# A third of the first projection by channel tiles, with the modulation weights in eight pieces

## What is computed

```
mod = silu(c) @ ada_w + ada_b                    # (1, 3072)
shift, scale, gate = split(mod, 3)
h = rms_norm(x, norm_g) * (1 + scale) + shift    # (1024, 1024)
p = h @ w_in                                     # (1024, 6152)
sb_q, sb_k, sb_v, ... = split(p)                 # 512 columns each
out = x + gate * (y @ w_out)                     # y: two attention branches, merged
```

## Time and profile before

| | us |
|---|---|
| median of 3 runs | 1090.92 |
| lowest, highest | 1087.15, 1091.58 |
| the profiled execution | 1092.36 |
| its span, first to last instruction | 1090.6 |
| mean granted TensorE clock, share of full | 0.945 |
| PE busy | 985.8 (90%) |
| DVE busy | 548.4 (50%) |
| ACT busy | 294.5 (27%) |
| POOL busy | 232.5 (21%) |

### The profile page before, as it was taken

The page is one execution under the profiler, slowest core; times in us unless marked ns, Lnnn a source line. Parts: engine busy times, 40 slices in busy tenths (PEclk is TensorE's granted clock), DMA queues, the critical chain, the costliest instruction groups (busy, mean ns, idle before and its releaser), DMA issues.

```text
span 1090.6 us, 14498 instructions
## 1 busy us (share of the span) xinstructions
PE 985.8 (90%) x5931; PEld 832.7 (76%) x5931; DVE 548.4 (50%) x768; ACT 294.5 (27%) x700; POOL 232.5 (21%) x112
## 2 busy tenths in 40 slices
PE   2279999869999899999979998899999969999998
PEld 2279999757787688888757886688888858788886
DVE  5888644667778344444034227033335472854522
ACT  2331111326777432122611100123233311111000
POOL 0241130060000021211213020200011253685000
PEclk9589999859999899999989998899999979999999
DMA  8906100231101112121221342511212944345331
GB/s 273 346 7 193 41 1 1 83 112 33 33 21 35 47 39 58 39 59 33 64 57 51 130 120 91 132 42 47 69 49 68 322 141 135 116 142 185 108 100 64
DMA packets 110763, 100.59 MB, mean 92 GB/s; under 512 B 17927, under 2 KB 90208, under 8 KB 110442
## 3 DMA queue, kind: packets, MB, share of 16 engines
q1 hardware_dynamic: 110698, 99.67, 30.0%
HBM read 73.44 MB, written 24.12 MB: 89 GB/s over the span
## 4 chain that ended last, share of the span: by engine, by line
PE 72%; DVE 10%; DMA 8%; ACT 3%; issue 3%; POOL 3%; SPq 1%; ACTq 0%; DVEq 0%
PE psum L688 32%; PE psum L263 7%; PE psum L264 7%; PE psum L265 7%; PE psum L902 3%; DMA sg<-z_scratch 3%; PE psum L887 3%; DMA w3raw<-in_w_in 2%; PE psum L873 2%; DMA ada<-in_ada_w 2%; DVE macc L465 1%; PE psum L875 1%; DVE blocks L1549 1%; PE psum L1216 1%; DVE stick L993 1%
## 5 line engine op out<-in xcount | busy, mean ns | idle before, releaser
L688 PE MATMUL psum<-hhi,w3hl 128*128 128x512 f32 x1152 | 389.4, 409 | 23.5 <-issue 19.6
L688 PEld LDWEIGHTS psum<-hhi,w3hl 128*128 128x128 f32 x1152 | 222.7, 193 | 74.6 <-issue 24.6
L688 PE MATMUL psum<-hlo,w3hl 128*128 128x512 f32 x576 | 229.6, 399 | 0.0
L678 POOL TENSOR_TENSOR w3hl<-w3raw,w3hl 128x1024 fp32r<-128x1024 f32 x44 | 107.5, 2444 | 536.5 <-DVE w3hl L672 536.5
L688 PEld LDWEIGHTS psum<-hlo,w3hl 128*128 128x128 f32 x576 | 111.9, 194 | 23.3 <-issue 2.2
L263 PE MATMUL psum<-w1hi,hhi 128*128 128x256 f32 (+1 forms) x384 | 110.4, 287 | 16.2 <-ACT hst L386 7.8
L672 DVE CAST w3hl<-w3raw 128x1024 fp32r<-128x1024 f32 x44 | 35.8, 814 | 157.8 <-DMA w3raw<-in_w_in 137.5
L264 PE MATMUL psum<-w1lo,hhi 128*128 128x256 f32 (+1 forms) x384 | 109.4, 285 | 0.0
L265 PE MATMUL psum<-w1hi,hlo 128*128 128x256 f32 (+1 forms) x384 | 109.3, 285 | 0.0
L993 DVE TENSOR_TENSOR_SCAN stick<-stick,zero 128x1024 f32<-128x1024 f32 (+7 forms) x64 | 91.8, 1473 | 19.1 <-ACT stick L945 18.9
L263 PEld LDWEIGHTS psum<-w1hi,hhi 128*128 128x128 f32 x384 | 74.1, 193 | 16.6 <-issue 16.6
(11 more groups left out here) (211 smaller groups left out, 1450.7 us busy)
## 6 DMA issues: line engine op xcount, KB each, us to landing
w3raw<-in_w_in SPq DMA_DIRECT2D x36, 512.0 KB, 4.2
z_scratch<-zst SPq DMA_DIRECT2D x48, 256.0 KB, 2.3
ada<-in_ada_w SPq DMA_DIRECT2D x8, 1024.0 KB, 8.3
sg<-z_scratch SPq DMA_DIRECT2D x8, 1024.0 KB, 4.9
w1raw<-in_w_in SPq DMA_DIRECT2D x6, 1024.0 KB, 6.8
xrow<-in_x SPq DMA_DIRECT2D x8, 512.0 KB, 7.5
adag<-in_ada_w SPq DMA_DIRECT2D x8, 512.0 KB, 4.1
zraw<-z_scratch SPq DMA_DIRECT2D x8, 512.0 KB, 6.3
```

Source lines behind the costliest of these rows:

```text
L678: nc.gpsimd.tensor_tensor(w3lo[:, i % 2], w3raw[:], cast(w3hi[:, i % 2]), ALU.subtract).then_inc(w3_lo, 1)
L688: t = nc.tensor.matmul(out_, a[:, i % 2, kt, :], moving[b][:, kt, 512 * half:512 * half + 512], start=(ends[0] and kt == k0 and m == 0), s ...
```

## The change

- `x` is loaded whole, in four loads of 1 MB, ahead of all weights; squared, scaled and turned whole, and kept turned in `hturn`, which lies where `hlo` will be. ACT copies it there from PSUM.
- The weights of shift and scale come in eight pieces, one for each channel tile (kt): 128 columns of shift and 128 of scale, two loads of 512 KB, in two buffers. For each, DVE makes a weighted sum 256 wide (`channel_sums`), PE two sums over partitions (`modulation`), and DVE shift and gain of that channel tile (`gains`).
- ACT makes h of a channel tile twice from `hturn` (128x1024): once in float32 and once as `hhi`. DVE makes the low part (`low_h`). POOL has nothing to do in phase 0.
- Chunks 0 and 1 are done together, 512 columns wide, by channel tile: seven row tiles in seven PSUM banks, then the eighth row tile alone. Bank 7 holds the modulation sums. Their weights come in two halves of the contraction; the high part is made by ACT (`high_w`), the low part by DVE (`low_w`).
- Chunk 2 has buffers of its own, where `hst` and `macc` were, and its low part is made by DVE. Chunks 3 to 5 go as before, with the other buffers; `high_1` of chunk 3 waits for the end of the first pair, `r_mm` 8.
- SP loads the weights of chunks 2 and 3 at the end of `sp_0`, those of 4 and 5 between the gate's weights.

```diff
+            for i in range(ST // 2):
+                sp.dma_start(xrow[:, 2 * i:2 * i + 2, :], x_v[:, 2 * i:2 * i + 2, :]).then_inc(x_in[i], 16)
+            def load_ada(kt):
+                if kt >= 2:
+                    sp.wait_ge(mod_part, kt - 1)
+                for part in range(2):
+                    n0 = D * part + P * kt
+                    sp.dma_start(ada[:, kt % 2, :, part], ada_v[:, :, n0:n0 + P]).then_inc(ada_in[kt % 2], 16)
+            load_ada(0)
+            for half in range(2):
+                for ch in range(2):
+                    kts = slice(KT // 2 * half, KT // 2 * (half + 1))
+                    sp.dma_start(w1raw[:, ch, kts, 0:256], w_v[:, kts, 256 * ch:256 * ch + 256]).then_inc(w1_in[half], 16)
+                if half == 0:
+                    load_ada(1)
+            for kt in range(2, KT):
+                load_ada(kt)
+            load_w1(sp, 2)
+            load_w1(sp, 3)
...
+            for half in range(2):
+                for kt in range(KT):
+                    for i in range(ST // 2):
+                        st = ST // 2 * half + i
+                        if kt == 0:
+                            pe.wait_ge(xn_ok, st + 1)
+                        if i == 0 and KT * half + kt >= FIRST:
+                            pe.wait_ge(xt_ok, KT * half + kt - FIRST + 1)
+                        t = nc.tensor.transpose(turned(half, kt)[:, P * i:P * i + P], xrow[:, st, P * kt:P * kt + P], ident[:, :])
+                    t.then_inc(xt_mm, 1)
+        def modulation(pe, kt):
+            pe.wait_ge(mod_part, kt + 1)
+            if kt:
+                pe.wait_ge(mod_ok, kt)
+            for part in range(2):
+                t = nc.tensor.matmul(bank(7)[:, part:part + 1], macc[:, kt % 2, P * part:P * part + P], ones[:, 0:1],
                                      start=True, stop=True)
             t.then_inc(mod_mm, 1)
...
+            def keep_turned(half, kt):
+                act.wait_ge(xt_mm, KT * half + kt + 1)
+                nc.scalar.copy(hturn[:, kt, 512 * half:512 * half + 512], turned(half, kt)).then_inc(xt_ok, 1)
+            def high_w(half):
+                act.wait_ge(w1_in[half], 32)
+                kts = slice(KT // 2 * half, KT // 2 * (half + 1))
+                nc.scalar.copy(w1hi[:, :, kts, 0:256], w1raw[:, :, kts, 0:256]).then_inc(w1_hi, 1)
+            def modulate(kt):
+                act.wait_ge(mod_ok, kt + 1)
+                act.wait_ge(xt_ok, KT + kt + 1)
+                if kt >= 2:
+                    act.wait_ge(hlo_ok, kt - 1)
+                for h in (hst[:, kt % 2], hhi[:, kt]):
+                    t = nc.scalar.activation(h, hturn[:, kt], ACT.Identity, bias=shift[:, kt:kt + 1],
+                                             scale=g1[:, kt:kt + 1])
+                t.then_inc(hf_ok, 1)
             norm(0)
             norm(1)
+            for kt in range(KT):
+                keep_turned(0, kt)
+            for kt in range(KT // 2):
+                keep_turned(1, kt)
+            high_w(0)
             modulate(0)
+            for kt in range(KT // 2, KT):
+                keep_turned(1, kt)
+            high_w(1)
+            for kt in range(1, KT):
+                modulate(kt)
...
+            def channel_sums(kt):
+                dve.wait_ge(ada_in[kt % 2], 32 * (kt // 2 + 1))
+                if kt >= 2:
+                    dve.wait_ge(mod_mm, kt - 1)
+                weighted_sum(dve, macc[:, kt % 2].rearrange("p (a b) -> p a b", a=2), ada[:, kt % 2], mod_part)
+            def gains(kt):
+                dve.wait_ge(mod_mm, kt + 1)
+                a, b = V_AB + KT + kt, V_AB + kt
+                nc.vector.tensor_tensor(shift[:, kt:kt + 1], bank(7)[:, 0:1], paramT[:, b:b + 1], ALU.add)
+                link(dve, dve_chain, nc.vector.tensor_tensor(ab1[:, kt:kt + 1], bank(7)[:, 1:2], paramT[:, a:a + 1], ALU.add))
+                nc.vector.scalar_tensor_tensor(out=g1[:, kt:kt + 1], in0=ab1[:, kt:kt + 1], scalar=1.0,
+                                               in1=paramT[:, V_NG + kt:V_NG + kt + 1], op0=ALU.add,
+                                               op1=ALU.mult).then_inc(mod_ok, 1)
+            def low_h(kt):
+                dve.wait_ge(hf_ok, kt + 1)
+                nc.vector.tensor_tensor(hlo[:, kt], hst[:, kt % 2], cast(hhi[:, kt]), ALU.subtract).then_inc(hlo_ok, 1)
+            def low_w(half):
+                dve.wait_ge(w1_hi, half + 1)
+                kts = slice(KT // 2 * half, KT // 2 * (half + 1))
+                nc.vector.tensor_tensor(w1lo[:, :, kts, 0:256], w1raw[:, :, kts, 0:256], cast(w1hi[:, :, kts, 0:256]),
+                                        ALU.subtract).then_inc(w1_lo, 1)
...
             scale_rows(dve, 0)
             scale_rows(dve, 1)
+            channel_sums(0)
+            gains(0)
+            channel_sums(1)
+            low_w(0)
+            for kt in range(KT):
+                low_h(kt)
+                if kt + 1 < KT:
+                    gains(kt + 1)
+                if kt + 2 < KT:
+                    channel_sums(kt + 2)
+                if kt == 1:
+                    low_w(1)
...
+        def slot_free(eng, ch):
+            if ch == 2:
+                eng.wait_ge(hlo_ok, KT)
+            else:
+                eng.wait_ge(r_mm, ST if ch < NCH - 1 else 3 * ST)
...
+        def first_chunks(pe):
+            def tile(st, kt):
+                w = [t[:, 0:2, kt, 0:256] for t in (w1hi, w1lo)]
+                return three(bank(st), hhi[:, kt, P * st:P * st + P], hlo[:, kt, P * st:P * st + P], w[0], w[1],
+                             kt == 0, kt == KT - 1)
+            modulation(pe, 0)
             for kt in range(KT):
+                if kt + 1 < KT:
+                    modulation(pe, kt + 1)
+                pe.wait_ge(w1_hi, 1 + (kt >= KT // 2))
+                pe.wait_ge(w1_lo, 1 + (kt >= KT // 2))
+                pe.wait_ge(hf_ok, kt + 1)
+                pe.wait_ge(hlo_ok, kt + 1)
+                for i in range(FIRST):
+                    st = (i + 2) % FIRST
+                    if kt == 0:
+                        pe.wait_ge(xt_ok, min(KT + 2 + i, 2 * KT))
+                    t = tile(st, kt)
                     if kt == KT - 1:
                         t.then_inc(r_mm, 1)
+            pe.wait_ge(mod_ok, KT)
+            for kt in range(KT):
+                t = tile(FIRST, kt)
+            t.then_inc(r_mm, 1)
         def pe_1(pe):
+            first_chunks(pe)
+            for ch in range(2, NCH):
                 pe.wait_ge(w1_hi, ch + 1)
                 pe.wait_ge(w1_lo, ch + 1)
+                for st in range(ST):
+                    n = (ch - 1) * ST + st
+                    pe.wait_ge(r_ok, n - 2 if ch == 2 and st < 4 else n - 3)
                     for kt in range(KT):
+                        w = [t[:, kt, 0:width_1(ch)] for t in (high_of(ch), low_of(ch))]
                         t = three(bank(n % 4)[:, 0:width_1(ch)], hhi[:, kt, P * st:P * st + P],
+                                  hlo[:, kt, P * st:P * st + P], w[0], w[1], kt == 0, kt == KT - 1)
                     t.then_inc(r_mm, 1)
+            pe.wait_ge(r_ok, ST)
...
+            for st in range(ST):
+                act.wait_ge(r_mm, st + 1)
+                t = (st + 2) % FIRST if st < FIRST else st
+                nc.scalar.copy(rows[:, 0, t, :], bank(t)).then_inc(r_ok, 1)
+            for n in range(ST, (NCH - 1) * ST):
+                ch, st = n // ST + 1, n % ST
                 act.wait_ge(r_mm, n + 1)
                 if ch == NCH - 1:
                     nc.scalar.copy(ba[:, st, :], bank(n % 4)[:, 256:256 + WB])
                 nc.scalar.copy(rows[:, ch // 2, st, 256 * (ch % 2):256 * (ch % 2) + 256],
                                bank(n % 4)[:, 0:256]).then_inc(r_ok, 1)
+                if n in (2 * ST + 3, 4 * ST + 3):
+                    act.wait_ge(ss1_ok, 1 if n < 4 * ST else 2)
...
-            high_1(dve, 1)
+            high_1(dve, 2)
+            low_2(dve)
+            high_1(dve, 3)
             dve.wait_ge(par1_in, 64)
             nc.vector.scalar_tensor_tensor(out=gain[:, 2], in0=gain[:, 0], scalar=float(HD) ** -0.5, in1=gain[:, 1],
                                            op0=ALU.mult, op1=ALU.mult)
             for g in range(GG // 2):
                 gate_sum(g)
-            high_1(dve, 2)
+            high_1(dve, 4)
             for g in range(GG // 2, GG):
                 gate_sum(g)
             dve.drain().then_inc(gacc_ok, 1)
-            dve.wait_ge(r_ok, 2 * ST)
-            high_1(dve, 3)
+            dve.wait_ge(r_ok, ST)
             squares(0)
             normalize(0)
-            high_1(dve, 4)
             high_1(dve, 5)
-            dve.wait_ge(r_ok, 4 * ST)
+            dve.wait_ge(r_ok, 3 * ST)
             squares(1)
             normalize(1)
```

More of the change, by code:

```diff
@@ L100, in hybrid_block @@
         hhi = kept("hhi", [P, KT, S], F32R)
+        hturn = Region(kept.at, kept.end)("hturn", [P, KT, S])
         hlo = kept("hlo", [P, KT, S], F32R)
```

(27 more changed lines are left out.)

156 lines of the change are left out of this document (38 added, 118 removed).

## The result

The ratio of the changed kernel to the one before is **0.9767 [0.9739, 0.9796]**: a median of 1064.03 us (1062.48 to 1068.55, 4 runs) against 1090.37 (1087.15 to 1091.58, 4 runs). That is 26.3 us less; 18.8 were forecast. Of one later run of the same kernel the profiled execution was disturbed (1621.9 us), so that run gives a ratio and no profile.

The account below looks back on a forecast made before the run. TensorE's late start, idle stretch and slow spells bound the first projection; 90.7 (first pair) + 91.5 (other chunks) + 3.0 (stall) + 2.0 (clock fall) + 5.1 (tail) = 192.3 against 211.07, -18.8, so 1072.1 us; range 1062 to 1084.

Parts of the forecast that it names:

- The start: TensorE's first projection tile begins at 36.4 us instead of 53.2, after x, turns, first sum and low parts.
- the second half's turns: 32 turns of the second half of x on TensorE, 0.161 us each, 5.2 in all, ending at 27.9.
- DVE's step: DVE's work per channel tile: 256-wide sum 4.0, low h 1.23, gains 0.5; together 5.7 us.
- The margin of 0.4: Per channel tile DVE's 5.7 us exceed TensorE's 5.3, so DVE binds the piecewise stage.
- Kt 0 and kt 2: First channel tile starts with 4 us of low clock; TensorE waits 2.7 us ahead of the third, and the clock falls.
- The new stall: In chunk 3 ACT stops for the squares of chunks 0 and 1: TensorE stalls 3.0 us, plus 2.0 for a clock fall.
- what comes behind is not edited: Everything after the first projection's end, the store of v, was taken as unchanged, so it added nothing to the forecast.
- A: Rival: DVE waits for modulation weights in each channel-tile step, 7.3 us instead of 5.7: 1082 us; chance 0.12.
- B: Rival: a channel tile's sums, gains, modulation and low part do not overlap: 1087 us, no change; chance 0.07 with D.
- C: Rival: TensorE stays at 1.2 GHz through the piecewise stage, 9.5 us per step: slower, 1104 us; chance 0.04.
- D: Rival: x or weights land so late that tiles start near 53 us: 1087 or so; chance 0.07 with B.

Follow-up runs that it names:

- its repetition: The changed kernel run once more, unedited, for a second undisturbed profile: ratio 0.9763, store of v at 192.22 us.
- x late: Changed kernel with the second half of x loaded behind the first two modulation-weight pieces and half the projection weights: 1078.09 us, 0.9889.
- the gate sums moved: Changed kernel with two of eight gate sums put ahead of the split of chunk 3's weights: 1058.49 us, 0.9704.
- quartered loads: Changed kernel with each modulation-weight piece in four loads of 256 KB instead of two of 512 KB: 1066.06 us, 0.9768.
- both fillers: Changed kernel with extra TensorE work in two idle stretches of the start: identity matmuls, 1071.58 us, or turns of x, 1065.01 us.
- identity variant: Changed kernel with 36 and 28 identity matmuls in TensorE's two idle stretches of the start: 1071.58 us, 0.9819.
- low part on GpSimd: Changed kernel with both low parts of the first pair's weights moved from DVE to GpSimd: 1065.7 us, 0.9765.

## Why the prediction was right, and where it was off

**The start.** 35.16 against 36.4. The term that was mis-sized is the second half's turns, priced at 0.161 each: 30 of them ran in the 3.5 us behind the last scaling (0.116 each), and they ended at 26.07 instead of 27.9. The squares were quicker too, at 1.04 to 1.06 each once x is there and not 1.28, but x landed 0.4 later, and the last one ended at 18.3, as forecast.

**DVE's step.** The 256-wide sum, priced linearly between the earlier trace rows at 4.0, took 3.99; low h 1.22 against 1.23. Gains took 0.33 with little between the instructions, so DVE's own step is 5.4 (62.34 to 67.72), not 5.7, and TensorE's is 5.3 as forecast. The margin of 0.4 by which DVE was to bind was not there: at kt 0 and kt 2 DVE waits for TensorE (2.97 and 1.78), and later the two wait for each other by turns, 0.3 each, with tiles 5.6 apart (63.70 to 74.83 for two).

**Kt 0 and kt 2.** The low clock at the start lasted 5.8 us, not 4 (35.2 to 41), so kt 0's tiles took 7.6 instead of 6.6, and ACT's two modulations took 2.4 and not 2.1. The earlier start paid for both: kt 2 came at 51.07, forecast 51.5. The wait of 2.52 and the fall behind it came as priced (the last matmuls of the pair end at 90.5; forecast 90.7). That these errors cancelled is luck. So is a part of the fall itself: behind the same wait the clock fell in four profiles (this one, its repetition, x late, the gate sums moved) and stayed up in three (quartered loads, both fillers). The prediction took the fall for a matter of the wait's length.

**The new stall** behind the squares: 3.36 against 3.0, and the clock fall 3.4 us at half pace, 1.7 against 2.0. It was found by asking what is queued behind `high_1`'s new wait. This fall, too, was not certain: at 3.19 and 3.29 of waiting in two variants there was none. Chunk 2's tiles leave each 2.88 instead of 2.84.

**The step that was off** is "what comes behind is not edited", priced at nothing: 5.2 of the 23.9 between the spans of the two profiled executions lie there. It isn't an effect of a fixed size: in eleven profiles of the changed kernel and its variants the stretch took 870.1 to 877.8, and in the one of before 879.5. But it isn't scatter alone. In three comparisons the unedited changed kernel's median is 26.3, 27.9 and 25.0 below that of before, so if 18.7 lie ahead of the meeting in every run, 6 to 9 lie behind it. The mean clock over the whole span points the same way: 0.946 to 0.959 in 25 executions of the kernel before that were run beside the experiments, 0.959 to 0.969 in 12 of the changed kernel, though a part of that lies ahead of the meeting (38 us at the low level before, 18 after). By the issue times of the same loads and stores, counted from the meeting, the kernel before is behind the changed kernel's repetition by 2.3 us at 184, 6.7 at 369, 7.6 at 642 and 10.0 at 722: it builds up in steps. The identity variant was 7.1 behind at 369 too, so such steps aren't bound to the kernel before. What makes them, and why that kernel has more of them, stays open; nothing was tried on it.

**The rivals.** A fell twice: no wait of DVE for a piece in the trace, and one wait of 0.89 with twice the loads. The page "DMA: Bandwidth & Descriptors" of the Trainium skill, section "Rules for kernel authors", asks for at least 1 MiB per load where bandwidth is to be highest; here loads of 512 KB, and even of 256 KB, cost next to nothing: they landed in 5.3 and 5.0 us (medians), and by the forecast's working 7.4 lie between issue and need. B fell: ACT's modulation lies within DVE's next sum, and a step took 5.6 us. C fell: 2.4 GHz from 41. "TensorE: Matmul & The Clock Gate", section "HAM oscillation — how this bites in real kernels", in the Trainium skill, warns of waiting between slices of the contraction; its case is a product of 128 rows, where a slice's work is shorter than the wait for the next. Here the work of a slice (5.3 us) is longer than any wait between slices. A cost of that kind shows in this trace behind the wait of 2.52 (0.57 in 51 to 55), and not behind those of 0.3; the wait of 3.36 (0.50 in 140 to 142) lies between tiles of later chunks. The experiment that takes the waits between slices away by having all of h first was 3.1% slower than the unedited kernel beside it (1095.94 to 1062.7). D fell: 35.16.

## What to carry to other kernels

A contraction can start before its operand is whole, if the producer's step is at most a little longer than the consumer's: here the overlap was worth 30 us, more than the whole gain. Put the producer's side work where it would wait anyway, and look at what is queued behind each new wait; moving two such things won 0.8% more. A wait of 2.5 us in front of TensorE was paid a second time in clock in four profiles of seven; price it as a chance, not as a certainty. A gain of 4 us can be read at a landmark in the trace when the median can't show it, but read a landmark close behind the edit: at the meeting, one clock fall more or less at the stall makes 1.7 us that the edit has no part in.

## What was not expected of the hardware

- Identity matmuls back to back did not hold TensorE's clock (0.85 in 32 to 34, 0.50 in 34 to 36, with PE busy for all 4 us); turns of x in the same place did (1.00 from 26 to 41).
- Idle times of 2.5 us ahead of kt 2 were followed by a clock fall in the changed kernel (51.07, [2.52]), its repetition (51.20), with the gate sums moved (50.38) and with x late (61.36), and by none with quartered loads (51.34, [2.53]), with identity matmuls (51.97, [2.52]) and with turns (48.73, [2.48]). At the squares there was a fall behind 3.12 (the repetition) and 3.36, and none behind 3.19 (low part on GpSimd) and 3.29 (x late). So the length of the idle time alone doesn't decide it.
- In the changed kernel the clock stood at 1.00 in every window from 0 to 30 us, though TensorE was busy for only 0.4 of the first 15.7; at the first tile, where it had idled for 2.5, it was at 0.50.
- The same code in the same kernel ran behind the meeting in 870.1 and in 874.3 us, with 58 and 68 us at the low level.
- A GpSimd subtraction of 128x2048 took 4.5 us and held one DVE step for its whole length (4.31 instead of 0.16).
